# Turning the scan's values, keys and factors with full-array transposes and half-partition copies

## The reference

```
def step(S, inp):
    r_t, w_t, k_t, v_t, a_t, b_t = inp
    sa = jnp.einsum('zbhvk,zbhk->zbhv', S, a_t)
    S = S * w_t[..., None, :] + sa[..., :, None] * b_t[..., None, :] + v_t[..., :, None] * k_t[..., None, :]
    return S, jnp.einsum('zbhvk,zbhk->zbhv', S, r_t)
```

## Time and profile before

| what | value |
|---|---|
| median of 3 runs | 1317.07 us (1314.99 to 1318.88) |
| the profiled execution, its own time | 1313.56 us |
| its span | 1311.7 us |
| PE busy | 1258.2 us, 96% of the span |
| ACT busy | 644.8 us, 49% |
| scan, tiles 0 to 7 | about 854 to 1070 us from the span's start |
| one tile of the scan (tiles 2 to 6) | 27.2 us |

### The profile page before, as it was taken

How to read it: one execution, slowest core, us unless ns; L and a number is a source line. 1 busy time by engine, 2 the same in 40 slices (tenths; PEclk the granted TensorE clock), 3 DMA queues, 4 the chain that set the end, 5 groups by cost and what they waited for, 6 DMA issues and landing times.

```text
span 1311.7 us, 30542 instructions
## 1 busy us (share of the span) xinstructions
PE 1258.2 (96%) x12736; PEld 1138.6 (87%) x12736; DVE 942.7 (72%) x1334; ACT 644.8 (49%) x1045; POOL 437.1 (33%) x220
## 2 busy tenths in 40 slices
PE   8999999999899999999999789989999999899998
PEld 5899999877889999889999689889999887799998
DVE  7677767786866777766667897686767656767775
ACT  5544456553554444645544456743444433644443
POOL 1244442312134444343344100173343413244442
PEclk9999999999999999999999789899999999999999
DMA  8345555422444455635544434110000013554553
GB/s 342 126 178 183 186 192 178 159 97 97 158 177 180 179 181 186 236 146 192 191 179 179 160 135 167 49 51 4 4 3 4 4 51 133 201 183 180 180 186 123
DMA packets 18667, 188.18 MB, mean 143 GB/s; under 512 B 2064, under 2 KB 2576, under 8 KB 3600
## 3 DMA queue, kind: packets, MB, share of 16 engines
q1 hardware_dynamic: 18576, 186.84, 39.1%
HBM read 185.78 MB, written 1.05 MB: 142 GB/s over the span
## 4 chain that ended last, share of the span: by engine, by line
PE 81%; DVE 13%; ACT 4%; issue 2%; DMA 0%; SPq 0%; DVEq 0%; ACTq 0%
PE gu_bank L257 22%; PE gu_bank L259 11%; PE bank L1381 7%; PE bank L236 7%; PE bank L238 7%; PE bank L237 7%; PE gu_bank L1400 5%; PE gu_bank L236 3%; PE gu_bank L238 3%; PE gu_bank L237 3%; DVE WL L193 2%; PE gu_bank L1381 2%; ACT WH L186 1%; DVE XSQ L407 1%; DVE HX L383 1%
## 5 line engine op out<-in xcount | busy, mean ns | idle before, releaser
L202 POOL TENSOR_TENSOR WL<-raw,WH 128x1024 fp32r<-128x1024 f32 x102 | 341.6, 3349 | 595.8 <-ACT WH L187 574.1
L257 PE MATMUL gu_bank<-HX,WH 128*128 128x512 f32 x1408 | 508.5, 403 | 11.9 <-DVE WL L193 10.2
L259 PE MATMUL gu_bank<-HX,WL 128*128 128x256 f32 x1408 | 398.1, 283 | 0.0
L193 DVE TENSOR_TENSOR WL<-raw,WH 128x2048 fp32r<-128x2048 f32 (+1 forms) x114 | 252.5, 2215 | 138.1 <-ACT WH L186 138.1
L257 PEld LDWEIGHTS gu_bank<-HX,WH 128*128 128x128 f32 x1408 | 267.7, 190 | 77.2 <-DVE WL L193 8.3
L259 PEld LDWEIGHTS gu_bank<-HX,WL 128*128 128x128 f32 x1408 | 269.0, 191 | 0.1
L186 ACT ACTIVATE WH<-raw 128x2048 fp32r<-128x2048 f32 (+1 forms) x114 | 204.6, 1795 | 23.3 <-PE gu_bank L238 13.5
L236 PE MATMUL bank<-PH,WH 128*128 128x256 f32 (+1 forms) x720 | 201.7, 284 | 1.0 <-ACT arena L1931 0.9
L237 PE MATMUL bank<-PL,WH 128*128 128x256 f32 (+1 forms) x720 | 201.6, 283 | 0.0
L238 PE MATMUL bank<-PH,WL 128*128 128x256 f32 (+1 forms) x720 | 201.5, 283 | 0.0
L438 ACT ACTIVATE work<-work 128x256 f32<-128x256 f32 x88 | 36.8, 418 | 303.1 <-DVE work L490 303.1
(11 more groups left out here) (307 smaller groups left out, 2012.2 us busy)
## 6 DMA issues: line engine op xcount, KB each, us to landing
raw<-stream_in SPq DMA_DIRECT2D x114, 1536.0 KB, 6.7
cst<-const_in SPq DMA_DIRECT2D x1, 1568.0 KB, 17.2
X<-xT_in SPq DMA_DIRECT2D x1, 1024.0 KB, 5.4
raw<-stream_in SPq DMA_DIRECT2D x1, 1024.0 KB, 7.4
arena<-hconst_in SPq DMA_DIRECT2D x2, 512.0 KB, 10.8
out<-X SPq DMA_DIRECT2D x4, 256.0 KB, 2.3
arena<-hconst_in SPq DMA_DIRECT2D x1, 768.0 KB, 13.9
arena<-fw_in SPq DMA_DIRECT2D x1, 512.0 KB, 8.2
```

What stands on the lines that cost most here:

```text
L193: nc.vector.tensor_tensor(WL[:, slot, :cut], raw[:, slot, :cut], WH[:, slot, :cut].bitcast(fp32), ALU.subtract).then_inc(lo_ready, 1)
L202: (eng or nc.gpsimd).tensor_tensor(WL[:, slot, cut:end], raw[:, slot, cut:end], WH[:, slot, cut:end].bitcast(fp32), ALU.subtract).then_inc ...
L257: nc.tensor.matmul(out[:, :], WH[:, slot, w:w + P], HX[:, x, :, :].rearrange("p i t -> p (i t)"), start=k == 0, stop=False)
L259: return nc.tensor.matmul(out[:, L:2 * L], WL[:, slot, w:w + P], HH[:, x, :], start=False, stop=k == CT - 1)
```

## The change

`pe_tr` takes a direction's 4 units with one pair of 64x64 products and three transposes of 128x128 (the full array, two neighbouring chunks' 64 columns each). A transpose of units u and u + 1 puts u's time in the lower and u + 1's in the upper partitions, with both heads side by side; of its four 64x64 blocks two are wanted, one in each half: the lower half keeps head 0 of u, the upper half head 1 of u + 1. The two blocks that no transpose makes are the pair's. Bank 7 takes direction 1 and, new, bank 5 direction 0 (the values, which have one direction, use bank 7). `act_tr` picks the wanted blocks with one activation for each half of the partitions and each bank, 64x256 each: 2 at level 0, 4 at levels 1 and 2.

At levels 1 and 2 the turning stands no longer between the units of `zee(n, 1)` but in front of them, and `act_tr` stands between ACT's copies of direction 0 and direction 1. `pe_spread` gets one more wait, on `tr_ready`, since it writes bank 5.

```diff
-        def pe_tr(pe, p, n, cs):
-            src = (VC, by_unit(KD[p]), by_unit(BB[p]))[n]
-            for c in cs:
-                last = heads(bank[7], at64(c), src[:, c], istack)
-            return last
+        def tr_banks(n):
+            return (bank[7],) if n == 0 else (bank[5], bank[7])
+        def pe_tr(pe, p, n):
+            src, lo, hi = (VC, by_unit(KD[p]), by_unit(BB[p]))[n], slice(0, HD), slice(HD, P)
+            for z, dst in enumerate(tr_banks(n)):
+                u = z * NCH
+                nc.tensor.matmul(dst[lo, 7 * CH:8 * CH], src[lo, u + NCH - 1], istack[lo], start=True, stop=True)
+                nc.tensor.matmul(dst[hi, 0:CH], src[hi, u], istack[hi], start=True, stop=True)
+            for z, dst in enumerate(tr_banks(n)):
+                for c in range(NCH - 1):
+                    u = z * NCH + c
+                    last = nc.tensor.transpose(dst[:, CH + c * P:CH + c * P + P],
+                                               src[:, u:u + 2].rearrange("p u t -> p (u t)"), ident)
+            last.then_inc(tr_done, 1)
...
+                if n in (1, 2):
+                    pe_tr_wait(pe, t, n)
+                    pe_tr(pe, p, n)
                 zee_wait(n, 1)
...
-                if n in (1, 2):
-                    pe_tr_wait(pe, t, n)
                 for c in range(NCH):
                     last = zee(n, 1, c)
-                    if n in (1, 2):
-                        tr = pe_tr(pe, p, n, (2 * c, 2 * c + 1))
                 last.then_inc(z_done, 1)
-                if n in (1, 2):
-                    tr.then_inc(tr_done, 1)
...
             dst = (VTK, KTK, BTK)[n][p]
-            src = bank[7][:, 0:(NCH if n == 0 else NU) * CH].rearrange("p (c s) -> p c s", s=CH)
-            nc.scalar.activation(dst[:, :, :], src, ACT.Copy).then_inc(tr_ready, 1)
+            for z, src in enumerate(tr_banks(n)):
+                for h in range(2):
+                    r = slice(HD * h, HD * h + HD)
+                    last = nc.scalar.activation(dst[r, z * NCH:(z + 1) * NCH, :],
+                                                src[r].rearrange("p (c o d) -> p c o d", o=2, d=HD)[:, :, 1 - h, :], ACT.Copy)
+            last.then_inc(tr_ready, 1)
...
                     A(zb, ZBANK[z][:, 0:P].rearrange("p (k b) -> p k b", b=LEVELS[n]), cp).then_inc(zb_ready, 1)
+                    if z == 0 and n in (1, 2):
+                        act_tr(act, t, p, n)
...
-                if n < 3:
+                if n == 0:
                     act_tr(act, t, p, n)
```

More of the change, by code:

```diff
@@ L1569, in pe_tile @@
                     pe_tr_wait(pe, t, 0)
-                    pe_tr(pe, p, 0, range(NCH)).then_inc(tr_done, 1)
+                    pe_tr(pe, p, 0)
                 if step:
@@ L2168, in pe_spread @@
             pe.wait_ge(gn_rec, 1 if j < CT - 2 else 2)
+            if j == 0:
+                pe.wait_ge(tr_ready, 3 * CT)
             if j == 2:
```

## The result

| | before | after |
|---|---|---|
| median of 7 runs each | 1317.88 us | 1325.16 us |
| lowest to highest | 1314.99 to 1318.88 | 1321.7 to 1326.22 |
| ratio | | 1.0053, 95% interval 1.0039 to 1.0066 |
| profiled execution, and its span | 1313.56, 1311.7 us | 1325.39, 1323.5 us |

A forecast was written before the change was run, and what follows sets the result against it. PE's order was taken to bound the steady tile; 4.5 us for tiles 1 to 7 plus 1.5 for tile 0 made 6.0, so 1317.07 became 1323.1 us. Its own range was 1320.8 to 1325.2, the full range 1316.5 to 1329.0.

The forecast's parts named there:

- PE's order binds the steady tile: In steady tiles, time added to PE lengthens the tile equally; ACT counts only if direction 1's copy delays `update(n, 1)`.
- The visit: Each turning on PE pays for changing to the full array and back: 0.27 us, bounds 0.18 and 0.35.
- The turnings: On PE, level 0 takes 0.72 us instead of 0.50; levels 1 and 2, with `zee(n, 1)`, 1.61 instead of 1.40.
- A steady tile: Each of tiles 1 to 7 gets 0.64 us longer: 0.22 at level 0, 0.21 at each of levels 1 and 2.
- ACT's copies: At levels 1 and 2, four half-partition copies start 0.33 us apart and take 1.37 instead of 0.60, covered in steady tiles.
- the room in front of `update(n, 1)`: Steady tile, level 1: ACT's direction 1 copy is ready 0.3 us early; cover goes if copies start over 0.41 apart.
- Tile 0: In the first tile, updates wait for ACT's direction 1 copy: +0.65 us at each of two levels, +0.22 at level 0, 1.5 together.
- The sum: Whole kernel: 4.5 us from tiles 1 to 7 plus 1.5 from the first tile, +6.0, giving 1323.1 us.
- The first, ACT as the bound: Steady tiles wait for ACT because half-partition copies start 0.50 us apart; 1329 us, chance 10%.
- The second, no cost: Weight loads and drains at PE's shape changes hide behind the transposes; 1316.8 us, no change, chance 17%.
- The third, transposes at the price of a record: On PE a transpose costs 0.03 us and not 0.11, so instruction count decides; 1312.2 us, faster, chance 6%.
- The fourth, the clock: Transposes count as idleness, giving each tile a 3.4 us stretch at half clock, 1.7 lost each; 1337 us, chance 5%.

The follow-up runs named there:

- e3: e1 with each direction of levels 1 and 2 turned by itself, five visits to the full array a tile instead of three; 1329.38 us, ratio 1.0102.
- e1: Kernel after, with ACT's copies of the turned units behind its copy of direction 1 at levels 1 and 2, as before the change; 1326.26 us, ratio 1.007.
- e8: e1 with level 0's two half copies moved behind ScalarE's scaled copies of s; 1323.19 us in one execution.
- e6: Kernel before, with only the activations cut into half-partition copies, pairs and order unchanged; 1320.32 us, ratio 1.0037.
- e7: Kernel after, with tile 0 alone turned by pairs and copied with one activation as before, the new order kept; 1322.79 us, ratio 1.0045.
- e9: Kernel after, with tiles 0 and 1 turned and copied as before, the new order kept; 1328.48 us in one execution.
- e10: Kernel after's order, with only tile 1 in the new form and all other tiles by pairs with one activation; 1316.65 us in one execution.
- e4: e1 with level 0's values turned by four pairs and copied with one activation, as before the change; 1323.28 us in one execution.
- e2: Kernel after's order alone, with turning by 64x64 pairs and one activation as before the change; 1315.32 us against 1316.68, ratio 0.9995.
- e5: Kernel after with one 128-partition activation a bank instead of two half copies, the upper half holding wrong blocks; 1320.23 us, ratio 1.0025.

## Why the prediction was right

**PE's order binds the steady tile.** Shown. What was put into PE's order or taken out of it came out in the tile: in e3 PE is busy 0.60 longer than in e1 and the tile takes 0.60 more, and the only waits of tile 3 are DVE's of before.

**The visit.** Forecast 0.27, measured 0.27 at level 0, 0.24 at level 1, and 0.05 more on the run behind each, 0.30 by e3. The transposes from start to start were forecast at 0.11 and are there. The turnings were forecast at 0.72 and, with `zee(n, 1)`, 1.61; they are 0.72 and 1.62. Against the exact starts of before this is +0.27 (with the slow pair behind it), +0.19 and +0.22. The prediction put the old part of level 1 at 1.40, where the starts in the earlier trace rows give 943.17 - 941.73 = 1.44. What was left out was the slow pair at level 0, 0.05.

**A steady tile.** Forecast +0.64, measured +0.78. Mis-sized by 0.05 at level 0, 0.07 by s (e8), and 0.02 of rest. The prediction counted the room of level 0's copies up to level 1's `pe_tr_wait` and said that the scaled copies of s wait for PE anyway; at level 0 they don't, and PE is released by them.

**ACT's copies.** Forecast 0.33 apart, measured 0.39, so the room in front of `update(n, 1)` was 0.09 us and not 0.3. It held, but only just.

**Tile 0.** Forecast +1.5, measured +3.3 in the profiled execution. The mechanism, two updates waiting for direction 1 by 0.9 each, is in the waits as forecast, but its price was too low: level 0 cost 0.28, level 1 0.99 and level 2 0.94, where 0.22, 0.65 and 0.65 were forecast, 2.2 in place of 1.5 before the clock fell. At each of levels 1 and 2 the half copies, 0.39 apart and not 0.33, are 0.18 of what was missing; the rest is small delays between one engine and the next. What was left out altogether is the clock: behind such waits it stays low for 10.2 us in place of 3.4, and the remaining 1.1 of tile 0 comes there. e6 shows this stretch without transposes.

**The sum.** Seven tiles of 0.78 are 5.5; with tile 0 at +3.3 and tile 1's second stretch, 1.6, that is 10.4, more than the medians' 7.3. The two belong to different executions, and how often an execution has the long stretches can't be told from one profile of each kernel. Nor do the medians settle what tile 0 is worth in them. e7, which leaves tile 0 as before, took 2.4 us less than after, but in another series; against before in its own series it lies 6.3 over, 1.0 less than after's 7.3. e6 points higher: its 3.6 less 1.0 for the steady tiles leaves 2.6. So the closeness of +6.0 to +7.3 is in part luck. The steady part was 1.0 too small, tile 0 was 0.7 too small before the clock, and the clock had no term; the profiled execution's 10.4 lies outside the 3.8 to 7.9 that the forecast's own bounds allow, and the median of 1325.16 only just inside them (1325.2).

**The rivals.** The first, ACT as the bound, is true in tile 0 alone: 0.39 is below its 0.41 for a steady tile. The second, no cost, is excluded by e3's 0.30. The third, transposes at the price of a record, by 0.11. The fourth, the clock, is partly true. Its steady form isn't: tiles 3 to 6 have 1.00, and so had layer 0. But with the new form in tile 1 a stretch at 0.50 comes that isn't there without it (e9, e10). The Trainium skill, TensorE: Matmul & The Clock Gate, Part 4, says that transposes don't count as busy in the same way; the fall behind three transposes in e10 agrees with it, the steady tiles with 15 transposes each at 1.00 don't show it. Nor does it explain e4 and e1, where the clock falls in the same place with pairs, or with nothing of the turning, between the wait and the fall. What brings the fall is open: it may be the transposes, the gaps at the change of shape, or how much PE had stood still shortly before (1.2 us in e10, 1.2 and 0.2 in e4 and e1). A kernel with full-array products in place of the transposes wasn't tried.

No version was faster than before; e2 can't be told from it. With visits as the price, a full-array transpose of 0.11 in place of a pair of 0.12 has nothing to pay them with.

## What to carry to other kernels

Count the time from start to start and not the instructions: here a steady tile lost 45 records and PE was busy 0.79 us longer in it, because each switch of the array from 64x64 to 128x128 and back cost 0.30 us. If work in another tiling must be laid into a small-tile loop, put all of it in one place. When an engine that isn't the bound gets longer copies, look at what stands behind them in its queue, in the first iteration above all, where nothing covers it.

## What the runs showed of the hardware that was not expected

- ScalarE's copies out of PSUM over 64 partitions followed each other 0.39 us apart (64x256, 0.378 each), in strided form (after) or contiguous (e6), and also where the second reads another bank than the first (863.33 and 863.72, after). Two of 128x256 start 0.28 apart (e5) and 0.33 before: they overlap, and the half-partition ones didn't.
- A wait of PE of about 1 us in the first tile was followed by 10.2 us at half clock (after, e1, e4, e6) or 13.7 (e3, e8) in place of 3.4, although PE was busy in nearly all of them (9.72 of 10.20 in after). The same 2.1 us wait for DVE at the start of tile 1 was followed by 3.4 us at half clock in e2 and by 6.8 in e5.
- The same wait of 1.2 us in tile 1 was followed by no fall in before, e2 and e9, which turn by pairs there, and by one of 3.4 us in e7 and e10, which have full-array transposes behind it. But e4, with pairs behind it, has the fall too (3.4 us), and e1 has it (6.8 us) before the turning begins.
